# Leaving out the zero quarter of triangular stationary matrices in the RWKV-7 mixer of a two-layer backbone

## The reference

```
sa = einsum('bhvk,bhk->bhv', S, a_t)
S = S * w_t[:, :, None, :] + sa[..., None] * b_t[:, :, None, :] + v_t[..., None] * k_t[:, :, None, :]
y_t = einsum('bhvk,bhk->bhv', S, r_t)
```

## Time and profile before

| | |
|---|---|
| median of 3 runs | 2008.52 us (1998.97 to 2010.54) |
| profiled execution | 2009.72 us |
| its span | 2007.9 us |
| mean granted TensorE clock | 0.886 |
| TensorE matmul busy | 1671.7 us, 83% of the span, 12348 instructions |
| TensorE weight load busy | 1333.1 us, 66% |
| VectorE busy | 1095.3 us, 55% |
| ScalarE busy | 663.2 us, 33% |
| GpSimd busy | 126.8 us, 6% |

### The profile page before, as it was taken

The page is one execution under the profiler, slowest core; times in us unless marked ns, Lnnn a source line. Parts: engine busy times, 40 slices in busy tenths (PEclk is TensorE's granted clock), DMA queues, the critical chain, the costliest instruction groups (busy, mean ns, idle before and its releaser), DMA issues. The chain is left out here.

```text
span 2007.9 us, 29880 instructions
## 1 busy us (share of the span) xinstructions
PE 1671.7 (83%) x12348; PEld 1333.1 (66%) x12348; DVE 1095.3 (55%) x1830; ACT 663.2 (33%) x1012; POOL 126.8 (6%) x140
## 2 busy tenths in 40 slices
PE   6998999586678777999999969899864688769996
PEld 4656776454577645888877757678643677569974
DVE  2383457874554445555452254745686745457655
ACT  4354324224120126312222263533335211253343
POOL 0000112000122000000000000000100412000000
PEclk8998998788787777999999989989887878689998
DMA  8310210464100032322222022112050000254441
GB/s 363 116 53 22 73 53 32 169 252 164 48 2 2 1 126 119 111 105 87 102 99 90 1 87 69 57 64 84 32 191 0 2 1 2 84 209 169 168 167 43
DMA packets 41174, 181.98 MB, mean 91 GB/s; under 512 B 4688, under 2 KB 5328, under 8 KB 33232
## 3 DMA queue, kind: packets, MB, share of 16 engines
q1 hardware_dynamic: 41040, 180.08, 24.4%
HBM read 179.01 MB, written 1.05 MB: 90 GB/s over the span
## 5 line engine op out<-in xcount | busy, mean ns | idle before, releaser
L225 PE MATMUL ps<-hr,wr 128*128 128x512 f32 (+1 forms) x704 | 240.4, 341 | 3.9 <-DVE wr L218 2.0
L226 PE MATMUL ps<-hr,wr 128*128 128x512 f32 (+1 forms) x704 | 237.4, 337 | 0.0
L227 PE MATMUL ps<-hr,wr 128*128 128x512 f32 (+1 forms) x704 | 237.3, 337 | 0.0
L225 PE MATMUL ps<-hr_in,wr_in 128*128 128x512 f32 (+1 forms) x544 | 223.3, 410 | 12.7 <-DVE wr_in L218 10.2
L226 PE MATMUL ps<-hr_in,wr_in 128*128 128x512 f32 (+1 forms) x544 | 210.8, 388 | 0.0
L227 PE MATMUL ps<-hr_in,wr_in 128*128 128x512 f32 (+1 forms) x544 | 210.3, 387 | 0.0
L218 DVE TENSOR_TENSOR wr<-pr,wr 128x2048 fp32r<-128x2048 f32 (+1 forms) x58 | 115.8, 1996 | 132.0 <-ACT wr L214 125.3
L225 PEld LDWEIGHTS ps<-hr_in,wr_in 128*128 128x128 f32 x544 | 110.3, 203 | 63.1 <-issue 33.9
L225 PEld LDWEIGHTS ps<-hr,wr 128*128 128x128 f32 x704 | 134.3, 191 | 23.1 <-DVE wr L218 6.9
L227 PEld LDWEIGHTS ps<-hr,wr 128*128 128x128 f32 x704 | 134.2, 191 | 13.8
L226 PEld LDWEIGHTS ps<-hr,wr 128*128 128x128 f32 x704 | 134.2, 191 | 13.5
(11 more groups left out here) (415 smaller groups left out, 3068.8 us busy)
## 6 DMA issues: line engine op xcount, KB each, us to landing
mix<-in_w_in SPq DMA_DIRECT2D x68, 512.0 KB, 3.3
pr<-in_w_up SPq DMA_DIRECT2D x28, 1024.0 KB, 4.8
pr<-in_ada_w SPq DMA_DIRECT2D x42, 512.0 KB, 6.6
mix<-in_w_up SPq DMA_DIRECT2D x16, 1024.0 KB, 4.8
ring<-in_ada_w SPq DMA_DIRECT2D x28, 512.0 KB, 4.3
pr<-in_w_down SPq DMA_DIRECT2D x14, 1024.0 KB, 4.8
pr<-in_ada_w SPq DMA_DIRECT2D x8, 1024.0 KB, 15.7
pr<-in_w_out SPq DMA_DIRECT2D x16, 512.0 KB, 7.8
```

Source lines behind the costliest of these rows:

```text
L225: nc.tensor.matmul(out, sh, mh, start=first, stop=False)
L226: nc.tensor.matmul(out, sh, ml, start=False, stop=False)
L227: return nc.tensor.matmul(out, sl, mh, start=False, stop=last)
```

## The change

The 16 products of L2021 and the 16 of L2027 are both replaced by a call of `triangular`. For each tile and head it does two products in place of one. The first takes all 128 rows and those 64 columns of the stationary matrix that have no zero quarter (`rows_of(1 - d)`), and writes these 64 partitions of the output. The second takes the other 64 columns (`rows_of(d)`) and of the rows only the half that isn't zero there, `rows_of(d)`, with the same half of the moving rows, and writes the other 64 partitions. Each product has 64 moving columns, as before. Order, banks, waits and signals around them stay. 128 products of the whole kernel (2 layers, 2 directions, 2 groups, 16 each) become 256.

```
+            def triangular(d, j, matrix, rows, bank):
+
+                for hd in range(HEADS):
+                    o = (j % 2) * 256 + hd * HD
+                    moving = rows[:, j * 256 + hd * HD:j * 256 + (hd + 1) * HD]
+                    nc.tensor.matmul(bank[rows_of(1 - d), o:o + HD], mat(matrix, j, hd)[:, rows_of(1 - d)], moving, start=True, stop=True)
+                    mm = nc.tensor.matmul(bank[rows_of(d), o:o + HD], mat(matrix, j, hd)[rows_of(d), rows_of(d)], moving[rows_of(d)],
+                                          start=True, stop=True)
+                return mm
...
                 for j in range(TILES):
-                    for hd in range(HEADS):
-                        mm = nc.tensor.matmul(ps[j // 2][:, (j % 2) * 256 + hd * HD:(j % 2) * 256 + (hd + 1) * HD], mat(AkT, j, hd),
-                                              vT[:, j * 256 + hd * HD:j * 256 + (hd + 1) * HD], start=True, stop=True)
+                    mm = triangular(d, j, AkT, vT, ps[j // 2])
                 mm.then_inc(S("pq"), 1)
                 pe.wait_ge(S("qp_out"), d + 1)
                 for j in range(TILES):
-                    for hd in range(HEADS):
-                        mm = nc.tensor.matmul(ps[2 + j // 2][:, (j % 2) * 256 + hd * HD:(j % 2) * 256 + (hd + 1) * HD], mat(XT, j, hd),
-                                              Qp[:, j * 256 + hd * HD:j * 256 + (hd + 1) * HD], start=True, stop=True)
+                    mm = triangular(d, j, XT, Qp, ps[2 + j // 2])
                 mm.then_inc(S("q"), 1)
```

## The result

The changed kernel takes 2065.26 us, the median of 4 runs (2061.25 to 2067.78), against 2008.78 us before (4 runs, 1998.97 to 2010.54). The ratio is 1.0277, with a 95% interval of 1.0252 to 1.0303: slower by 56.5 us. The profiled execution, of 2061.25 us, is the fastest of the four, and its span is 2059.5 us, 51.6 us more than before. Of all executions shown here one is in a slow state, 2807.11 us of e3_keys_only at a mean clock of 0.545, and it is left out of every median and ratio.

A forecast was written before the change was run, and what follows sets the result against it. The fourth mixer was taken as a relay with one engine working at a time, so product time is kernel time. AkT +18.1 us and XT +26.0 make +44.1, 2052.6 against the median, written as 2053 us; range 2036 to 2075.

The forecast's parts named there:

- Nothing hides the two groups: AkT (L2021) and XT (L2027) products, 39.1 us together: a microsecond more or less in either is one of the kernel.
- The change of row count drains: Between parts of 128 and 64 rows TensorE finishes one first; the readout's two transitions a block cost 0.29 us together.
- The price of a part: Each part in both groups: 0.26 us at 2.4 GHz or 0.41 at 1.2 GHz; a product 0.52 or 0.82.
- The XT passes at 12.4 us: L2027's four passes: start at 2.4 GHz, clock falls after about 1.4 us, 12.4 us each, +26.0 us in all.
- The AkT passes at 2.4 GHz, 33.6 us: L2021's four passes: clock stays at 2.4 GHz, 8.4 us each against 15.5 in all before, +18.1 us.
- rival C: All passes at 1.2 GHz, up to 2075 us; second case, clock falling mid pass, 2063; everything above 2060: chance 32%.
- Rival A, side by side: Both groups: a product's two parts run together in different PSUM halves, 20.7 us less, 1989 us; chance 3%.
- GpSimd, queue and signals at no cost: Around both groups: 256 further matmul instructions in TensorE's queue, unchanged signals and GpSimd's wait for XT cost nothing.
- The sum: Whole kernel: +18.1 us in the AkT passes and +26.0 in the XT passes, +44.1 us.

The follow-up runs named there:

- e3_keys_only: Only the AkT products (L2021) in parts as in the change, XT products as in the kernel before: 2039.31 us, ratio 1.0155 to before.
- e1_full_rows: The changed kernel with all 128 rows kept in both parts, the zero quarter multiplied again: 1974.61 us, ratio 0.9823 to the kernel before.
- e4_inverse_only: Only the XT products (L2027) in parts as in the change, AkT products as in the kernel before: 2022.88 us in a single run.
- e8_twice: e1_full_rows with every part issued twice, the second writing the same result again: 1991.61 us, ratio 0.9933 to the kernel before.
- e2_grouped: The changed kernel's parts reordered: in each group all 16 of 128 rows, then all 16 of 64: 2004.56 us, ratio 0.9979 to before.

## Why the prediction was right, and where it was off

- **Nothing hides the two groups.** Right: they grew by 51.4 us and the span by 51.6; in e3_keys_only it is 31.3 us in the passes and 31.7 in the median.
- **The change of row count drains.** Right, and shown by the runs, since in the prediction it rested on the readout's rows: the same parts cost 61 us less in another order, and with all rows kept 91 us less. The readout's two transitions had cost 0.29 us together, and one change measured 0.14 us. In all these rows a change of row count is also a change of column half. A change of half alone costs nothing that shows (0.032 us from one instruction to the next in e1_full_rows); a change of row count within one half was not run.
- **The price of a part**, 0.26 or 0.41 us, 0.52 or 0.82 a product. Right: 0.513 and 0.81 measured for a product.
- **The XT passes at 12.4 us.** Too low by 0.6 us each, 2.3 in all. The step was right where its premise held: e4_inverse_only took 11.8 to 12.6. The premise failed, because behind the changed AkT pass there is no stretch at 2.4 GHz left.
- **The AkT passes at 2.4 GHz, 33.6 us.** This is the step that failed: they took 38.6 us. The argument was that TensorE is never idle in them and that the readout kept its clock through transitions. The readout has runs of eight and four instructions with 128 moving columns between its transitions, the passes have runs of two with 64. The clock fell in mid pass in all four. This is rival C's second case, "if the clock falls in mid pass, 2063"; the prediction gave everything above 2060 a chance of 32%. That 2063 comes within 3 us of the measured 2065.26 is in part luck. The prediction does not work it out: it comes out if half of the 19.2 us that the AkT passes would lose by 1.2 GHz throughout is put on top of the forecast. The passes as measured, 51.4 us more, make 2060 on the prediction's base of 2008.5. I had seen that clock as tied to the idle 1.45 us. e1_full_rows and e8_twice, which kept their clock across that gap in eight XT passes of eight, show that it is not the gap alone.
- **Rival A, side by side.** Wrong for the change, since the two parts differ in row count. With that difference taken away it is what happens: the estimate of 1989 was even too high, as it left the clock where it was.
- **GpSimd, queue and signals at no cost.** Nothing in the changed trace speaks against it: GpSimd is busy 126.8 us as before, and the span grew by what the passes grew.
- **The sum.** 44.1 us forecast, 51.4 in the passes, 56.5 in the medians. The 7.3 us between the first two are in the main the clock's, 5.0 in the AkT passes and 2.3 in the XT passes. The last 5 us lie between the medians and the profiled executions, not in the passes. The measured time is 12 us above the point forecast, and the range holds it because it went up to rival C.

What stays open: which property of the stream of parts lowers the clock. The runs vary its order, its density and its width together, and even within e2_grouped one XT pass kept the clock and three did not.

## What to carry to other kernels

Leaving out zeros in a stationary matrix saved nothing here, because it gave neighbouring products different row counts: each change of row count cost 0.14 us at 2.4 GHz and 0.19 at 1.2 GHz here; at 2.4 GHz that is more than half of a whole 128-column product, 0.227 us. With the zeros kept and the matrix split by columns into two halves of one row count, the same product took 0.13 us instead of 0.23. Where a change moves TensorE's clock, price the stretch behind it too, at the clock that it gets: here that was 10 of the 33 us won.

## What the runs showed of the hardware beyond that

A product of 128 rows by 128 stationary columns and 64 moving ones is dearer than its two column halves issued one after the other: 3.79 us against 2.03 us for 16, both at 2.4 GHz, with twice the instructions. The prediction had the price of such pairs from L2055 but did not look for the gain in the kernel.
